# First input chunk by halves, memory weights ahead of the experts, an earlier split between attention heads, and a tenth expert block ahead: four edits to a two-layer transformer kernel

## The reference

```python
# layer one
mod = silu(c) @ w_ada + b_ada                       # c: (1, 1024); six pieces of 1024
shift1, scale1, gate1, shift2, scale2, gate2 = split(mod, 6)
h = rms_norm(x, norm1_g) * (1 + scale1) + shift1
proj = h @ w_in                                     # (256, 5120): q, k, v twice, two gates
...                                                 # two attentions, branches, w_out, residual
scores = sigmoid(h2 @ w_router)                     # 64 experts, 8 for each token
x = x + gate2 * (sum_e w_e * swiglu_e(h2) + swiglu_shared(h2))     # FF 256
# layer two
u = rmsnorm(final_norm(x), g) @ w_in_2              # conv inputs, latents, gate logits
y_mla = softmax(q_nope @ k_nope.T + q_rope @ k_rope.T) @ v @ w_mla_out    # 8 heads
x = x + (g_conv * y_conv + g_mla * y_mla) @ w_mix_out
kv = rmsnorm(mem, g) @ w_mem_kv                     # mem: (256, 1024); keys 1024, values 1024
x = x + softmax(q @ k.T) @ v @ w_mem_out            # 4 heads of 256
gates, idx = top_k(softmax(h @ w_router_2).T, 32)   # 16 experts, 32 tokens each, FF 1024
x = x + scatter(gates * (silu(xg @ w_gate) * (xg @ w_up)) @ w_down)
```

## Time and profile before

| | us |
|---|---|
| median of 3 runs | 1632.26 |
| lowest, highest | 1630.64, 1637.18 |
| the profiled execution, its own time | 1639.27 |
| its span in the trace | 1637.1 |
| PE busy in it | 1348.4 (82%) |
| DVE, ACT busy | 554.4, 406.7 |
| DMA, mean rate | 320 GB/s of 523.33 MB |

### The profile page before, as it was taken

One profiled execution on the slowest core, in us unless ns is written; L12 is line 12 of the kernel. 1 busy time (PEld: TensorE's weight loads), 2 busy tenths in 40 slices (PEclk: granted clock), 3 DMA queues, 4 the chain that ended last, 5 costly groups with the idle time before them and its releaser, 6 DMA issues.

```text
span 1637.1 us, 22361 instructions
## 1 busy us (share of the span) xinstructions
PE 1348.4 (82%) x9064; PEld 852.7 (52%) x9064; DVE 554.4 (34%) x1214; ACT 406.7 (25%) x625; POOL 68.9 (4%) x140
## 2 busy tenths in 40 slices
PE   5899989899998798997799899999765556566566
PEld 2788887545444255453487899999412112112112
DVE  1446765443223133122474565654301001001001
ACT  2347752111111111110253336453200000000002
POOL 1940000000000000000000000000000000000000
PEclk8899999999999899998999999999788878879777
DMA  9994258799899999999933343546799999999995
GB/s 355 301 292 174 103 205 345 280 414 381 361 417 395 417 394 417 421 385 388 372 142 122 135 145 116 204 157 245 319 417 415 421 415 415 422 415 416 422 414 213
DMA packets 126217, 523.33 MB, mean 320 GB/s; under 512 B 12504, under 2 KB 16752, under 8 KB 84656
## 3 DMA queue, kind: packets, MB, share of 16 engines
q1 hardware_dynamic: 121408, 518.68, 80.0%
q0 software_dynamic: 4576, 2.95, 0.8%
q10 hardware_dynamic: 144, 0.44, 0.1%
HBM read 520.96 MB, written 1.06 MB: 319 GB/s over the span
## 4 chain that ended last, share of the span: by engine, by line
PE 58%; SPq 20%; DMA 13%; DVE 4%; issue 3%; ACT 1%; DVEq 0%; ACTq 0%; PEldq 0%
PE psum L1873 18%; PE psum L2265 11%; SPq L607 11%; SPq L603 8%; DMA ring<-in_w_up_e_dram 7%; PE psum L2313 4%; PE psum L2219 3%; DMA ring<-in_w_exp_down_dram 3%; PE psum L2208 2%; DVE ring_r L1054 1%; PE psum L1886 1%; PE psum L2549 1%; PE psum L2075 1%; PE psum L2243 1%; PE psum L2241 1%
## 5 line engine op out<-in xcount | busy, mean ns | idle before, releaser
L1873 PE MATMUL psum<-arena_r,ring_r 128*128 128x256 f32 x2592 | 323.4, 285 | 22.1 <-DVE arena_r L1061 8.7
L1873 PEld LDWEIGHTS psum<-arena_r,ring_r 128*128 128x128 f32 x2592 | 314.1, 192 | 31.3 <-issue 19.8
L2265 PE MATMUL psum<-ring,arena 128*32 128x512 f32 (+1 forms) x1152 | 188.7, 631 | 41.3 <-DMA ring<-in_w_up_e_dram 33.1
L1054 DVE TENSOR_TENSOR ring_r<-ring,ring_r 128x1024 fp32r<-128x1024 f32 x140 | 163.1, 1219 | 98.0 <-ACT ring_r L702 97.0
L2685 PE MATMUL psum<-ring,arena 128*32 128x512 f32 x752 | 115.0, 752 | 65.6 <-DMA ring<-in_w_exp_up_dram 63.4
L702 ACT ACTIVATE ring_r<-ring 128x1024 fp32r<-128x1024 f32 x140 | 137.5, 1049 | 53.7 <-DMA ring<-in_w_in_dram 34.9
L2265 PEld LDWEIGHTS psum<-ring,arena 128*32 128x32 f32 (+1 forms) x1152 | 57.7, 126 | 154.9 <-issue 153.9
L2703 PE MATMUL psum<-ring,arena 128*32 128x512 f32 x384 | 66.7, 829 | 49.1 <-DMA ring<-in_w_exp_down_dram 46.2
L2685 PEld LDWEIGHTS psum<-ring,arena 128*32 128x32 f32 x752 | 23.9, 124 | 148.3 <-DMA ring<-in_w_exp_up_dram 99.9
L2313 PE MATMUL psum<-ring,arena 128*32 128x512 f32 (+1 forms) x576 | 92.9, 610 | 2.1 <-DVE arena L1458 2.1
L1817 DVE TENSOR_TENSOR arena<-arena,psum 128x256 f32<-128x256 f32 x16 | 6.7, 421 | 254.4 <-ACT arena L1012 254.4
(11 more groups left out here) (401 smaller groups left out, 1407.3 us busy)
## 6 DMA issues: line engine op xcount, KB each, us to landing
ring<-in_w_gate_e_dram SPq DMA_DIRECT2D x64, 1024.0 KB, 11.5
ring<-in_w_up_e_dram SPq DMA_DIRECT2D x64, 1024.0 KB, 13.4
ring<-in_w_down_e_dram SPq DMA_DIRECT2D x64, 1024.0 KB, 13.9
ring<-in_w_exp_down_dram SPq DMA_DIRECT2D x96, 512.0 KB, 15.6
ring<-in_w_exp_gate_dram SPq DMA_DIRECT2D x47, 1024.0 KB, 25.8
ring<-in_w_exp_up_dram SPq DMA_DIRECT2D x47, 1024.0 KB, 26.3
ring<-in_w_in_dram SPq DMA_DIRECT2D x20, 2048.0 KB, 8.8
ring<-in_w_ada_dram SPq DMA_DIRECT2D x12, 2048.0 KB, 16.4
```

Of the source, the lines that this page charges most:

```text
L1054: V.tensor_tensor(lo, whole, hi.bitcast(F32), ALU.subtract).then_inc(w_low, 1)
L1873: ins = product(lambda a_, b_, k, first, last: mm(ps[:, t * T:(t + 1) * T], a_[:, k, c], b_[:, k, :], start=first, stop=last), w, x, arriving)
L2265: ins = mm(psum[c, 5, :], xg1[:, k, P * j + width * b:P * j + width * (b + 1)], gate[e][:, :, k, :], start=(k == 0), stop=(k == KT - 1))
```

## The change

- **First chunk.** `w_ada` chunks come in the order shift, scale, shift, scale for features 0 to 511 and then 512 to 1023 (`ADA_ORDER`). The columns of chunk n are turned before the matmuls of chunk n + 1. DVE modulates four tiles after two chunks and four after the other two. `w_in` chunk 0 is loaded by two DMAs of 1 MB, with a semaphore each. PE projects it by halves of the features: first features 0 to 511 for both outputs, then the rest.
- **Memory weights.** The first block is issued before the first expert pair, into buffers 4 and 12, and waits for the last attention output. Keys come first, then values. The pieces go to passes 8, 9, 11, 14, 17, 18, 20 and 21 in place of 6, 8, 10, 12, 14, 16, 18 and 20. A small table (`order`) moves to another buffer.
- **Latent attention.** For the first pair of heads ACT and DVE split the chunk of fill 2 and fill 3 ahead of their softmax work; DVE empties fill 2 before it splits the next chunk.
- **Tenth block.** In the first turn of MoE 2 a tenth block goes into buffers 8 and 1 (`parted`), once the last transpose of the routed activations (`gN3`) is done. The blocks from the eleventh on wait for what the tenth and later waited for.

```diff
-PIECE_AT = {6 + 2 * _u: _u for _u in range(PIECES)}
+PIECE_AT = {_p: _u for _u, _p in enumerate((8, 9, 11, 14, 17, 18, 20, 21))}
...
+ADA_ORDER = (0, 2, 1, 3) + tuple(range(ADA_FIRST, ADA))
-CHUNKS_A = [("w_ada", 512 * _j, 512, 8) for _j in range(ADA_FIRST)]
+CHUNKS_A = [("w_ada", 512 * ADA_ORDER[_j], 512, 8) for _j in range(ADA_FIRST)]
...
-        kv_w = [buf(i).rearrange("p (k c) -> p k c", k=4) for i in (4, 7)]
+        kv_w = [[buf(i).rearrange("p (k c) -> p k c", k=4) for i in (4, 7 if c else 12)] for c in range(PIECES // 2)]
-        order = buf(4, S_WIDTH, 1024)
+        order = buf(10, S_WIDTH, 1536)
...
         once = buf(5, SLOT)
-        ONCE = RING2
+        parted = (buf(8), buf(1))
+        ONCE, PARTED = RING2, RING2 + 1
...
+                elif spec == CHUNKS_A[IN_A[0]]:
+                    dst = ap.rearrange("p (k c) -> p k c", k=k)
+                    for h, landed in enumerate((first_in, done)):
+                        sp.dma_start(dst[:, 4 * h:4 * h + 4, :], a[name][0, 512 * h:512 * h + 512, 0:cols].rearrange("(k p) c -> p k c", p=P))\
+                          .then_inc(landed, 16)
...
                 if c:
                     sp.wait_ge(kv_made, 2 * c)
+                else:
+                    full(sp, f"av{PAIRS - 1}")
...
+            memory_weights(0)
             pair(0, (E1 - 4, E1 - 3))
             pair(3, (E1 - 2, E1 - 1))
             sp.wait_ge(table_ready, 1)
-            memory_weights(0)
...
                 if c == ONCE:
                     full(sp, "mla3")
-                elif c > ONCE:
-                    sp.wait_ge(used_b, NB + c - RING2 + (c > 2 * RING2))
+                elif c == PARTED:
+                    full(sp, "gN3")
+                elif c > PARTED:
+                    sp.wait_ge(used_b, NB + c - RING2 - 1 + 2 * (c > 2 * RING2 + 1))
...
             rms_act(1, rstd_of(1))
-            for n in range(ADA_FIRST):
+            for n in range(3):
                 ada_copy(n)
-            high(0, (0,))
-            for half in range(2):
-                act.wait_ge(normed, half + 1)
-                x_high_part("h1", half)
-                high(0, (1,) if half == 0 else (2, 3))
+            act.wait_ge(normed, 1)
+            x_high_part("h1", 0)
+            ada_copy(3)
+            high(0, (0, 1))
+            act.wait_ge(normed, 2)
+            x_high_part("h1", 1)
+            high(0, (2, 3))
...
             for p in range(HEADS // 2):
                 h0, h1 = 2 * p, 2 * p + 1
+                if p == 0:
+                    high(kb + 4)
                 latent_exp(h0)
                 latent_exp(h1)
-                high(kb + 4 + h0)
+                high(kb + 5 if p == 0 else kb + 4 + h0)
...
+            for half in range(2):
+                dve.wait_ge(mod_full, 2 * half + 2)
+                part = lambda ap: ap[:, 0:NF].rearrange("p (a c) -> p a c", a=2)[:, :, 4 * half:4 * half + 4]
+                V.tensor_tensor(part(mod), part(psum[:, 7, :]), part(vcols("b_ada")), ALU.add).then_inc(mod_ready, 1)
...
+                x_low_part("h1", half)
+                low_part(0, (0, 1) if half == 0 else (2, 3))
...
             for n in range(ADA_FIRST):
+                if n:
+                    if n == 3:
+                        pe.wait_ge(mod_ready, 1)
+                    columns(n - 1).then_inc(mod_full, 1)
                 modulation(n, n)
             columns(ADA_FIRST - 1).then_inc(mod_full, 1)
...
+            def project_by_halves(w):
+
+                hi, lo = PARTS["h1"]
+                for half in range(2):
+                    for j in range(2):
+                        name = f"in0_{j}"
+                        ps = bank(name) if half else start(name)
+                        for t in range(2):
+                            c = slice((2 * j + t) * P, (2 * j + t + 1) * P)
+                            for k in range(4 * half, 4 * half + 4):
+                                if j == 0 and t == 0 and k % 2 == 0:
+                                    pe.wait_ge(x_low, 4 * PART_AT["h1"] + k // 2 + 1)
+                                    pe.wait_ge(w_low, k // 2 + 1)
...
```

More of the change, by code:

```diff
@@ L473, in slot2 @@
                 return once, load_once, 0
-            j = ORDER2[(c - (not first or c > ONCE)) % RING2]
+            if first and c == PARTED:
+                return None, load_parted, 0
+            j = ORDER2[(c - 2 * (not first or c > PARTED)) % RING2]
             if j == "first added":
@@ L2680, in moe2_turn @@
                         arrived_moe2(pe, i, c, n)
-                        w = slot2(c, not n)[0].rearrange("p (g k f) -> p g k f", g=2, k=2)
+                        w = [half.rearrange("p (k f) -> p k f", k=2) for half in gate_and_up(c, not n)]
                         for k in range(2):
```

90 lines of the change are left out of this document (53 added, 37 removed).

## The result

The changed kernel takes 1618.69 us (median of 4 runs, 1616.76 to 1619.56) against 1634.62 us (4 runs, 1630.64 to 1637.18) of the kernel before: a ratio of 0.9899, with a 95% interval of 0.9881 to 0.9917, or 16.5 us with 13.6 to 19.5. It is faster, by less than the 22.4 us that the sum gave. The spans split into stages as follows. Each boundary is a start of PE in its timeline: the second pass of MoE 1, the first transposes behind its last gates, the first gates of MoE 2, the last down block.

The account below looks back on a forecast made before the run. It took DMA as the bound in the first 60 us, MoE 1 and MoE 2, and PE's order between the mixtures. Gains 5.3 + 4.5 + 7.6 + 5.0 = 22.4 us off 1632.3 gave 1610, range 1604 to 1619.

Parts of the forecast that it names:

- Latent, 7.6: Latent attention: PE's two waits and a slow fill go, next scores at 911.5 for 919.2, gain 7.6 us.
- Tenth block, 5.0: MoE 2: a tenth block loads in idle DMA time, every later one lands one block sooner, gain 5.0 us.
- Start, 5.3: First projection by halves: PE starts 5.6 us sooner, ends at 53.4; gain 5.3 us, later chunks moving along.
- the floor of 7.0: Start: an end of the first projection before 51.6 is useless, next chunk bounds; gain ends at 7.0 us.
- Rival 1: Start: the clock rises at the same moment as before, gain 2.3 for 5.3, time 1613; chance 0.17.
- MoE 1, 4.5: Passes 6 and 7 without pieces: 4.5 of the 6.7 us of DMA lost between 400 and 430 recovered.
- The cover of 20 against 19 us: MoE 1, four-expert passes with a piece: four freed slots keep DMA busy 20 us, PE needs 19; just covered.
- rival 2: MoE 1: DMA idle returns behind the four-expert passes, gain 0 for 4.5, time 1614.5; chance 0.18.
- Its pass of 13.6: MoE 1: a two-expert pass without a piece takes about 13.6 us of PE, against 15 us of DMA.
- Rivals 3 and 4: 3: two of four edits don't pay, 1618.5, chance 0.10; 4: pieces in four-expert passes starve the DMA, 1645, chance 0.03.
- What would show it: All four stages: the trace signs expected if right, such as first projection ending between 51.6 and 54, MoE 2 5.0 shorter.
- the signs of being wrong: DMA shares of 0.6 behind four-expert passes; clock low beyond 47 at start; stretch between mixtures not 7.6 shorter.

Follow-up runs that it names:

- run 6: The changed kernel with all pieces in two-expert passes (9, 10, 12, 13, 15, 16, 18, 19): 1606.91 us, ratio 0.9840 against the kernel before.

## Why the prediction was right, and where not

The number held, and in part by luck. 1618.7 lies in the range of 1604 to 1619, 0.3 from its end, and faster was given 0.92. But two of the four terms, 9.8 of the 22.4 us, did not show in the time; the range reached this far only because it took in the rivals and 2 us for the medians. Against the 1610 of the forecast the time is 8.7 longer: 2.4 of it is the median of the kernel before, 1634.6 over four runs for 1632.3 over three, and 5.9 the gain, 16.5 for 22.4. The four single edits multiply to 0.9904 against 0.9899, so within the intervals the gains do add.

- **Latent, 7.6:** right. 7.9 to the next scores; 9.6 (6.2 to 12.9) by time, where a later slow projection was gone too, which the clock gave and not the edit. (919.2 less 911.5 is 7.7, not 7.6.)
- **Tenth block, 5.0:** right to the tenth (442.9 to 437.8). The DMA runs at 421 to 423 GB/s there. The Trainium skill ("HBM Reference", section "Specifications (TRN2)") says that a core which streams alone gets about 425 GB/s, the measured rate, where the page that the prediction weighed gives 358.
- **Start, 5.3, measured nothing to 2.9:** the failed step is "Later chunks are asked for when a projection ends, so their arrival moves along with it". Chunk 2 was asked for 7.7 sooner and landed 2.4 sooner, because the DMA had been idle only for some 3 us before it (share 0.67 over 10 us) and now some 3 MB stand ahead of it in the queue: the memory columns and a modulation chunk. The forecast for the first projection was too careful: it ended at 50.9 for 53.4, since the clock rose 3.3 us after its start and not 7.65 (a number that the trace of before gives as 7.3). It made no difference, the floor of 7.0 being at the next chunk. Rival 1 did not happen as written.
- **MoE 1, 4.5, measured 0:** the step that failed is the last sentence on it, that the waits and the slow gates "stay, moved to other passes", with no price of their own. They became six instead of four. With no piece in passes 6 and 7 PE waits 3.62 ahead of pass 8 for 1.65, and with one piece instead of two since pass 14 it waits 11.62 ahead of pass 17 for 0.72; these are the two new slow ones. Each of the six costs 1.7 to 3.5 us of idle DMA, 16.0 for 10.6, and that takes back what passes 6 to 8 gained. The cover of 20 against 19 us, on which rival 2 was argued, was no issue: the idle comes before the piece. So rival 2 had the outcome (0.18) and the wrong reason. (Its pass of 13.6 is what the trace shows, while the three parts named add to 13.3.)
- **Rivals 3 and 4** did not happen: the latent edit and the tenth block both paid, and no pass cost the DMA a whole piece (3.5 us of 7.0 at most).
- **What would show it:** no wait above 1 us in the first projection (one of 1.24 ahead of it, none inside), DMA shares of 0.85, 0.99, 1.00 at passes 6 to 8, no waits at fill 2 and the next scores, and 5.0 in MoE 2: all seen. "An end of the stage 4.5 closer to its start" was not, and the first projection ended ahead of its 51.6 to 54. Of the signs of being wrong the first all but came: behind pass 14 the share is 0.65 from 560 to 570, and 0.20 in 4 us of it, where the sign names 0.6 and no length.

The Trainium skill ("TensorE: Matmul & The Clock Gate", section "HAM oscillation — how this bites in real kernels") describes a matmul loop whose every step starts cold behind a wait for the DMA, and counts the price as time of PE. The trace agrees on the cold gates (8.4 to 10.0 for 7.1). What they cost here is another thing: about 2 us each of a DMA queue that has no slot (16.0 less 3.4 over six places), and nothing where slots are free (run 6, pass 12).

## What to carry to other kernels

Where transfers are the bound, look at who holds their buffers when they stop: a wait of the "fast" engine ahead of the step that frees most buffers is not free if that step then runs at half the clock, and moving other work in front of it (or even useless work of the right length) gave 10 to 12 us here, while deleting 49 us of work gave nothing. The fillers pay only if they end when the block lands: twice as long, they cost 17 us. When a load is to come sooner, count the bytes ahead of it in its queue, not only the moment at which it is asked for. And compare stages between marks in the traces: 25 runs of the kernel before span 1630.8 to 1637.8, while T repeats within 0.5.
